# A two-layer streaming encoder step on one core: layers written out, row turns signalled in halves, loads reordered

## The reference, cut to what matters

```
q, k, v, r_q, r_k, r_v, r_g, c = split(x @ w_in[l])              # 1024 -> 3584 columns
mix = concat(diff_attention, retention, conv) @ w_out[l]
x = layer_norm(ALPHA * x + mix)                                  # first norm
gates = best group of 4 experts, then the top 2 inside it        # 16 experts, shared router
f = sum_e gates[e] * (silu(x @ w_gate[l, e]) * (x @ w_up[l, e])) @ w_down[l, e]
x = layer_norm(ALPHA * x + f)                                    # second norm
x = x + sigmoid(x @ w_ple_gate[l] + b_ple_gate[l]) * (p[l] @ w_ple_proj[l])   # side gate
```

## Time and profile before

| what | us |
|---|---|
| median of 3 runs | 1602.93 (1602.1 to 1605.95) |
| the profiled execution, its own time | 1602.15 |
| its span, first to last instruction | 1600.3 |
| TensorE busy | 1434.2 (90%) |
| VectorE busy | 582.0 (36%) |
| ScalarE busy | 269.4 (17%) |
| GpSimd busy | 96.8 (6%) |
| mean granted clock of TensorE, share of full | 0.962 |

### The profile page before, as it was taken

One profiled execution on the slowest core, in us unless ns is written; L12 is line 12 of the kernel. 1 busy time (PEld: TensorE's weight loads), 2 busy tenths in 40 slices (PEclk: granted clock), 3 DMA queues, 4 the chain that ended last, 5 costly groups with the idle time before them and its releaser, 6 DMA issues.

```text
span 1600.3 us, 20932 instructions
## 1 busy us (share of the span) xinstructions
PE 1434.2 (90%) x6898; PEld 754.5 (47%) x6898; DVE 582.0 (36%) x1173; ACT 269.4 (17%) x654; POOL 96.8 (6%) x133
## 2 busy tenths in 40 slices
PE   7999997998899999966979999979979999977588
PEld 3786456554344444323447854555543444323244
DVE  5095864345111011105611958553451111000156
ACT  2101343212100010000221023431121101000012
POOL 1100001000000000003000000010000000000110
PEclk9999998999999999997989999989999999999889
DMA  8532011353499889994032321013433899999911
GB/s 289 218 119 97 11 43 57 132 183 131 189 381 388 341 333 394 427 419 183 1 122 70 116 82 52 2 68 150 187 112 138 301 329 357 427 427 426 335 71 51
DMA packets 81957, 326.42 MB, mean 204 GB/s; under 512 B 12668, under 2 KB 15156, under 8 KB 56540
## 3 DMA queue, kind: packets, MB, share of 16 engines
q1 hardware_dynamic: 67636, 278.53, 45.4%
q0 software_dynamic: 9136, 29.16, 4.9%
q10 hardware_dynamic: 5112, 17.80, 2.8%
HBM read 429.25 MB, written 30.19 MB: 287 GB/s over the span
## 4 chain that ended last, share of the span: by engine, by line
PE 48%; issue 35%; DMA 8%; DVE 4%; POOL 2%; ACT 1%; DVEq 1%; SPq 1%; ACTq 0%; POOLq 0%
PE psum L1243 18%; PE psum L1270 9%; PE psum L1115 7%; DMA region<-in_w_exp_up_dram 5%; PE psum L1304 4%; PE psum L1244 2%; PE psum L1224 1%; PE psum L1143 1%; PE psum L1069 1%; DMA bias_sample_rows<-bias_rows 1%; PE psum L1100 1%; POOL rr L732 1%; PE psum L1271 1%; ACT xT L1515 1%; PE psum L837 1%
## 5 line engine op out<-in xcount | busy, mean ns | idle before, releaser
L1243 PE MATMUL psum<-ring,xT 128*64 128x512 f32 x800 | 357.7, 599 | 30.1 <-ACT xT L1515 10.9
L1244 PE MATMUL psum<-region,xT 128*64 128x512 f32 x800 | 358.7, 601 | 0.0
L1243 PEld LDWEIGHTS psum<-ring,xT 128*64 128x64 f32 x800 | 107.8, 138 | 234.4 <-issue 234.4
L1270 PE MATMUL psum<-ring,region 128*64 128x512 f32 x400 | 176.7, 593 | 12.4 <-issue 6.0
L1271 PE MATMUL psum<-region 128*64 128x512 f32 x400 | 177.0, 593 | 0.0
L892 PE MATMUL psum<-xT,ring 128*128 128x272 f32 x768 | 176.5, 393 | 0.0
L892 PEld LDWEIGHTS psum<-xT,ring 128*128 128x128 f32 x768 | 145.8, 190 | 30.1
L2047 DVE COPY region<-psum 128x512 f32<-128x512 f32 x25 | 17.3, 691 | 351.0 <-PE psum L1271 351.0
L951 PE MATMUL psum<-ring,xT 128*128 128x512 f32 (+1 forms) x288 | 135.9, 616 | 7.3 <-DVE region L1703 7.2
L1304 PE MATMUL psum<-ring,xT 128*128 128x512 f32 x256 | 115.3, 608 | 1.5 <-issue 1.5
L1270 PEld LDWEIGHTS psum<-ring,region 128*64 128x64 f32 x400 | 54.1, 137 | 116.7 <-issue 116.7
(11 more groups left out here) (263 smaller groups left out, 1498.4 us busy)
## 6 DMA issues: line engine op xcount, KB each, us to landing
region<-in_w_exp_gate_dram SPq DMA_DIRECT2D x54, 1024.0 KB
ring<-in_w_exp_gate_dram SPq DMA_DIRECT2D x54, 1024.0 KB
region<-in_w_exp_up_dram SPq DMA_DIRECT2D x54, 1024.0 KB
ring<-in_w_exp_up_dram SPq DMA_DIRECT2D x54, 1024.0 KB
ring<-in_w_exp_down_dram SPq DMA_DIRECT2D x54, 1024.0 KB
region<-in_w_exp_down_dram SPq DMA_DIRECT2D x54, 1024.0 KB
ring<-in_w_in_dram SPq DMA_DIRECT2D x24, 1024.0 KB, 8.6
expert_results<-region ACTq DMA_DIRECT2D x25, 512.0 KB, 7.9
```

The costliest lines, as they stand in the source:

```text
L1243: pe.matmul(bank[b][front, :], xeT[:, kc, front], ring[:, BLOCK_SLOT[u], kc % 4, :], start=kc == 0, stop=kc == KC - 1)
L1244: m = pe.matmul(bank[b][last, :], xeT[:, kc, last], back[:, UNIT_ROOM[u], kc % 4, :], start=kc == 0, stop=kc == KC - 1)
L1270: pe.matmul(bank[5 + half][front, :], hT[:, 2 * n + q, front], ring[:, BLOCK_SLOT[u], 2 * q + half, :], start=n + q == 0, stop=n + q == 2)
```

## The change

1. On TensorE, ScalarE, VectorE and GpSimd the loop over the layers becomes a Python loop: both layers are written out and `l` is a constant.
2. The turn of tile 0 for the next layer's input moves ahead of the sample tile's side gate on TensorE, and its copy ahead of `sample_out` on ScalarE. `bank_plan` gets three idle steps ahead of the `x2` turns, so that this turn's banks differ from those of the uses that it passes. SyncE waits for the last `pg` bank itself; `ring_free` is gone.
3. The turned rows of a round are signalled in halves: `xe_low_turned` behind the fourth transpose lets ScalarE copy bank 0.
4. The first round's conditional loads for gate and up go ahead of the back's early down weights and their waits.
5. The second norm's rows and the gate's bias are loaded at the start of the expert rounds, the rows into a free part of `xT` (`lnp_near`) from where ScalarE copies them to their place in two copies of 128x1024 ahead of the last round's `hidden_half`; the bias goes into `rt`'s room.
6. The side gate's second two units (`n` = 1) wait for the first tile's gathers, and the next layer's first two `in` units for the last tile's.

```diff
-    late += [("x2", 0, 0), ("x2", 0, 1)]
+    late += [None] * 3 + [("x2", 0, 0), ("x2", 0, 1)]
...
-        bple, at = part(at, D)
...
+        bple, _ = part(at, D)
         rt, at = part(at, 24, 80)
...
+        lnp_near = flat[:, 2 * D:4 * D].rearrange("p (a d) -> p a d", a=2)
...
+            def ring_left(l):
+
+                key = ("pg", TILES - 1, 1)
+                if l > 0:
+                    hold(full[use(key)], taken(l - 1, key) + 1)
...
-                        hold(ring_free, l + 1)
+                        ring_left(l)
...
+                if l > 0:
+                    for n in range(2):
+                        hold(yg_full[0][n], 16 * 2 * l)
                 for u in UNITS[:2]:
                     unit(u)
...
-                hold(ring_free, l + 1)
+                ring_left(l)
...
-                key = ("pp", 4, 1)
-                hold(full[use(key)], taken(l, key) + 1)
-                hold(xe_full, 16 * (base + 1))
-                for n in range(2):
-                    early("down", n, 1)
-
...
                 for name in ("gate", "up", "down"):
+                    if name == "down":
+                        key = ("pp", 4, 1)
+                        hold(full[use(key)], taken(l, key) + 1)
+                        hold(xe_full, 16 * (base + 1))
+                        for n in range(2):
+                            early("down", n, 1)
                     for n in range(2):
                         hold(b_full[BLOCK_SLOT[(name, n)]], 16 * (base + l + 1))
                         hold(z_full[BLOCK_SLOT[(name, n)]], 16 * (base + l + 1))
                     if name != "down":
                         part_of(name, 0)
+                e.dma_start(lnp_near[:, 0, :], a["ln2_g"][L].to_broadcast([P, D])).then_inc(ln2p_in, 16)
+                e.dma_start(lnp_near[:, 1, :], a["ln2_b"][L].to_broadcast([P, D])).then_inc(ln2p_in, 16)
+                e.dma_start(bple, a["b_ple_gate"][L].to_broadcast([P, D])).then_inc(ln2p_in, 16)
                 with e.Fori(0, mid) as k:
...
                 hold(gate_full, base + mid + 1 + 1)
-                e.dma_start(lnp[:, 0, :], a["ln2_g"][L].to_broadcast([P, D])).then_inc(ln2p_in, 16)
-                e.dma_start(lnp[:, 1, :], a["ln2_b"][L].to_broadcast([P, D])).then_inc(ln2p_in, 16)
-                e.dma_start(bple, a["b_ple_gate"][L].to_broadcast([P, D])).then_inc(ln2p_in, 16)
                 for u in UNITS[BEFORE_BLOCKS:BEFORE_BLOCKS + 2]:
                     unit(u)
                 hold(up_full, base + mid + 1 + 1)
+                for n in range(2):
+                    hold(yg_full[0][n], 16 * (2 * l + 1))
                 for u in UNITS[BEFORE_BLOCKS + 2:]:
                     unit(u)
...
-            with pl.Fori(0, DEPTH) as l:
+            for l in range(DEPTH):
...
-            with pe.Fori(0, DEPTH) as l:
-
-                turn_tile(l, "x0", x_ready, 0)
+            for l in range(DEPTH):
+
+                if l == 0:
+                    turn_tile(l, "x0", x_ready, 0)
...
                     for q in range(KC):
                         m = pe.transpose(bank[q // 4][:, (q % 4) * P:(q % 4 + 1) * P], xe[:, q::KC], ident[:])
+                        if q == 3:
+                            m.then_inc(xe_low_turned, 1)
                     m.then_inc(xe_turned, 1)
...
                         if n == 0 and t + 1 < TILES:
                             turn_tile(l, "x2", x2_ready, t + 1)
-                key = ("pg", TILES - 1, 1)
-                pe.wait_ge(full[use(key)], taken(l, key) + 1)
-                pe.sem_inc(ring_free, 1)
+                    if t == TILES - 2 and l + 1 < DEPTH:
+                        turn_tile(l + 1, "x0", x_ready, 0)
...
-            with sc.Fori(0, DEPTH) as l:
+            for l in range(DEPTH):
+                def x0_turned(l, t):
+                    for s in range(2):
+                        key = ("x0", t, s)
+                        take(l, key, xT[:, 4 * s:4 * s + 4, span(t)], quad(B(key), ROWS[t]))
...
-                    sc.wait_ge(xe_turned, base + k + 1 + 1)
+                    sc.wait_ge(xe_low_turned, base + k + 1 + 1)
...
+                sc.wait_ge(ln2p_in, 48 * (l + 1))
+                for n in range(2):
+                    sc.activation(lnp[:, n, :], lnp_near[:, n, :], ACT.Copy).then_inc(ln2p_home, 1)
                 hidden_half(mid)
                 result(mid)
...
                 gates(sc, l, TILES - 2)
+                if l + 1 < DEPTH:
+                    x0_turned(l + 1, 0)
                 for n in range(2):
                     sample_out("pg", n)
...
-            with ve.Fori(0, DEPTH) as l:
+            for l in range(DEPTH):
...
                 ve.wait_ge(ln2p_in, 48 * (l + 1))
+                ve.wait_ge(ln2p_home, 2 * (l + 1))
```

More of the change, by code:

```diff
@@ L364, in encoder_step @@
         w_full = [sem(f"slot_full{i}") for i in range(SLOTS)]
-        ring_free = sem("ring_free")
         b_full = [sem(f"front_slot_full{i}") for i in range(SLOTS)]
@@ L379, in encoder_step @@
         ln2p_in = sem("ln2p_in")
+        ln2p_home = sem("ln2p_home")
         ple_in = sem("ple_in")
@@ L449, in encoder_step @@
         xe_full = sem("xe_full")
+        xe_low_turned = sem("xe_low_turned")
         xe_turned = sem("xe_turned")
@@ L1352, in _ @@
                 sc.dma_start(dst, src).then_inc(biasc_in, 16)
-            for signal in (*free, ring_free, out_k, out_c, o_done, silu_done, h_done, ye_done, y_out, gate_full, up_full, gate_read, up_read, *dn_full, xe_turned):
+            for signal in (*free, out_k, out_c, o_done, silu_done, h_done, ye_done, y_out, gate_full, up_full, gate_read, up_read, *dn_full, xe_low_turned, xe_turned):
                 sc.sem_inc(signal, 1)
@@ L1372, in _ @@
                 for t in range(TILES):
-                    for s in range(2):
-                        key = ("x0", t, s)
-                        take(l, key, xT[:, 4 * s:4 * s + 4, span(t)], quad(B(key), ROWS[t]))
+                    if t > 0 or l == 0:
+                        x0_turned(l, t)
                     if t > 0:
```

## The result

| | before | after |
|---|---|---|
| median, us | 1602.51 (1601.2 to 1605.95, 4 runs) | 1577.03 (1573.96 to 1579.39, 4 runs) |
| ratio to before, 95% interval | | 0.9827 (0.981 to 0.9844) |
| profiled execution, us (span) | 1602.15 (1600.3) | 1573.96 (1572.0) |
| mean granted clock of TensorE | 0.962 | 0.967 |

The change gains 25.5 us by the medians and 28.2 by the two profiled executions; 31.1 had been forecast. On a second chip the same kernel took 1579.64 us where before took 1603.56, 23.9 less. So some 3 to 7 us of the sum did not come.

What follows compares the result with a forecast made beforehand. TensorE, busy 1434.2 of 1600.3 us, bounds the kernel, so only its idle stretches and lower clock can move the time. Terms 11.4 + 8.1 + 3.9 + 7.7 = 31.1 off 1602.15 give 1571.0; range 1561 to 1586.

Steps and rivals of the forecast that it cites:

- 1575.5: Total if DMA queues take turns packet by packet at the tail: held weights bring only 1.2 us a layer, sum 26.6.
- (2): Tails: the last result write and gather do not profit, their 6.2 us belong to the write; 1579 us, chance 0.12.
- (3): Expert rounds: weight loads bound the shorter rounds sooner and the 7.7 us are lost; 1579 us, chance 0.12.
- (4): Seam between layers: the stall stays, as the second code copy must be fetched; 9 of 11.4 us stay, 1580, chance 0.08.
- rival 1: The forecast's own sum of all terms, 31.1 us gained; chance 0.53.
- The seam: Between the layers: loops written out and tile 0 turned early save 9.4 us of gap and 2.0 of clock, 11.4.
- The tails: End of each layer: early norm rows and held side-gate weights speed the last write and layer one's root; 8.1 us.
- The halves of the turn: Expert rounds: ScalarE's copy, signalled after four transposes, lets the gate start 0.45 us sooner in 17 rounds; 7.7 us.
- Constants in the waits: Inside a layer: constants replacing registers in waits, taken as 0, between a loss of 1 us and a gain of 4.
- The first round: First expert round of each layer: gate loads issued ahead of down weights gain 2.1 and 1.8 us, together 3.9.
- (5): Hand-overs in both layers: registers in waits cost more than seen, 10 us more gained; 1561 us, chance 0.10.
- (6): Unlooped stretches of both layers: longer straight code stalls in fetching, 4.04 us per stall, making it slower; chance 0.03.

Runs made afterwards that it cites:

- the repaired kernel: Changed kernel with SyncE's waits for the early down weights' landing moved behind the next round's gate loads: 1573.27 us (ratio 0.9802), repeated on another chip 1573.55 (0.9822).

## Why the prediction was right, and where it was not

The forecast was 1571.0 us with a range of 1561 to 1586; the time was 1577.03. By the number alone that is nearer to 1575.5, to rivals (2) and (3) at 1579 and to (4) at 1580 than to the forecast, 6.0 us away. The experiments speak for its own sum (rival 1), with one term lost. Point by point:

- **The seam**: 11.4 forecast; 11.8 in the changed kernel's trace (L866's first product at 811.66 becomes 794.53, 17.13 sooner, and the next turn behind it, at 819.00, becomes 799.78, 19.22 sooner, of which 7.41 were there at the side gate); 10.0 by the medians when it was done alone. Right as a sum. Of the parts, the jump is worth more (6.6 of the gap) and the turn less than the idle times of the earlier trace rows suggested: ScalarE's table load went with the jump too.
- **The tails**: 8.1 forecast; 5.0 and 4.0 in the two layers of the changed kernel, 9.8 by the medians when they were done alone. Right, and by the mechanism: the write's 7.04 us became 3.41 to 3.43 in both layers, 3.6 each. Which load crowds the write was put down to the rows and the weights together; the runs divide it, the held weights in layer one, mostly the rows in layer two.
- **The halves of the turn**: 7.7 forecast, 7.9 in the stretches, 8.6 by the medians. Right, down to the last rounds left out.
- **Constants in the waits**: 0 forecast, and outside the seam no stretch of the kernel with only the loops written out is shorter.
- **The first round**: 3.9 forecast, and here the step failed. It said: "The down weights go out some 3 us later, for use 20 us on: nothing." They went out 6.4 us later (408.09 for 401.65), since SyncE works through both the gate's and the up's loads first. TensorE's use of them is still late enough. But SyncE itself waits for their landing, in order, ahead of round 1's gate loads. The later issue moved that landing to 417.0 us, the gate loads to 421.97 and round 1 by 4.3 us. For the tail's new wait the forecast did name what is queued behind it; for this one it did not. The tail's cost of the norm's rows in round 0 was put at nothing, too, and their 1.3 us of issuing stand in the same queue. The gain was oversized as well: the 3.34 and 2.34 us of idle time in the earlier trace rows were those of one execution. In five others with the old order, where layer one's turn 0 came at 405.3 to 406.8 and not at 401.6, gate(0) had at most 0.99 us ahead of it in layer one and 1.04 in layer two. One of the forecast's own signs of being wrong so came true: more waits for expert weights, eight for five, if not longer ones.

The seam, the tails, the halves and the order, each alone, bring 10.0 + 9.8 + 8.6 + 3.3 = 31.7 us by their medians. Together they brought 25.5 and 23.9, and with the new wait removed 31.2 and 30.0 on two chips. So the 6 to 8 us that are lost in the whole are about what the wait costs there by the medians. The account does not close to the microsecond: the order alone has the wait too, only shorter, and its 3.3 us by the medians are a loss of 0.5 in its rounds. That the repaired kernel's gain comes so near to the forecast's 31.1 is in part luck: the order's 3.9 are not borne out by the rounds, and the tails and halves came out 1.7 and 0.9 us above their terms by the medians, the seam 1.4 below.

The rivals: the write and the gather did profit (2 falls). The weights bound the last rounds only, 1.5 us (3 falls as a whole). The seam kept no stall (4). The registers cost nothing that shows (5): no stretch outside the seam got shorter. And no straight stretch has a new stall (6): in the kernel with only the loops written out, TensorE's longest gap without a releaser outside the tails is 3.60 us ahead of L1061, and the kernel before stood 3.87 us there as well.

Open: what the repaired order of the first round is worth, and why the stretch up to turn 0 takes 400.2 to 407.1 us. A part of that scatter lies near its end: from the first product of L1205 (seats of the rows, its line before) to turn 0 it is 7.2 to 10.2 us.

## What to carry to other kernels

When a transfer is issued later, look at who waits for its landing, and then at what that engine's queue does next: here the user of the data had 20 us to spare and the issuing engine had none. Put a wait for a landing directly ahead of the first instruction that needs it. And before a gain is counted from an idle time at the start of a stage, ask whether the engine is always that early; a stretch that scatters by 7 us makes a poor base for a term of 2. Last, when two parts of a change put work into one engine's queue, price them together: the norm's issues did no harm alone, and behind the new wait they made it longer.

## What the hardware showed beyond expectation

- With the loop written out the gap at the seam was 6.6 us shorter, more than the 4.04 that TensorE's own idle row named: ScalarE stood 5.05 and then loaded its table for 1.28, and in the straight code neither is there.
- Behind a stop of 2.65 us in the middle of dense work the granted clock read 0.54 and 0.51 for the next 3.6 us, which added 1.7 us to the wait. Behind one of 1.40 us at the same place, in the kernel of the order alone, it stayed at 1.00.
- The same 512 KB write took 3.4 us from issue to the gather that waits for it with the DMA engines half free, 4.4 in layer two when the side gate's weights were not held, and 7.05 in layer one with the engines full.
